# Hybrid decoder step on one core: rate products of layer 0 at earlier steps, two state stores moved behind the last

## The reference, cut to what matters

```python
mod = (silu(c) @ w_ada[0] + b_ada[0])        # shift, scale, gate rates: 6 x 2048 per sequence
sh1, sc1, g1, sh2, sc2, g2 = split_cols(mod, [D_MODEL] * 6)
h = rms_norm(x, norm_mix) * (1 + sc1) + sh1
z = h @ ev_w_in                              # 2048 x 4112
q, k, v, r, a_lr, u = split_cols(z, ...)
o, s_new = gated_linear_recurrence(q, k, v, log_a, s)   # s: one 128 x 256 state per head, 4 heads
p = multiscale_pool(u, ...)                  # windows 2, 4, 8, 16, then a 256 x 256 product per group
x = x + g1 * (concat([rms_norm(o) * silu(r), p]) @ ev_w_out)
```

## Time and profile before

| | |
|---|---|
| median of 3 runs | 2540.3 us (2539.91 to 2542.41) |
| profiled execution, its own time | 2540.4 us |
| its span (first to last instruction) | 2538.6 us |
| PE / PEld busy | 2498.6 us (98%) / 2420.8 us (95%) |
| DVE / ACT / POOL busy | 1509.9 / 985.5 / 157.5 us |
| DMA over the span | 620.50 MB, mean 244 GB/s |
| mean granted TensorE clock | 0.996 |

### The profile page before, as it was taken

The page is one execution under the profiler, slowest core; times in us unless marked ns, Lnnn a source line. Parts: engine busy times, 40 slices in busy tenths (PEclk is TensorE's granted clock), DMA queues, the critical chain, the costliest instruction groups (busy, mean ns, idle before and its releaser), DMA issues.

```text
span 2538.6 us, 59285 instructions
## 1 busy us (share of the span) xinstructions
PE 2498.6 (98%) x24993; PEld 2420.8 (95%) x24993; DVE 1509.9 (59%) x2265; ACT 985.5 (39%) x1144; POOL 157.5 (6%) x211
## 2 busy tenths in 40 slices
PE   7999999999999999999999999999999999999998
PEld 6888799999999999999999999999999999999998
DVE  4575555554454455445548999996755654654654
ACT  3243343332333332333335565656433333333333
POOL 1000331000000000000020020300000000000011
PEclk9999999999999999999999999999999999999999
DMA  9999989899999998998655474745555555555553
GB/s 351 371 353 323 325 303 311 274 311 313 302 311 304 307 309 299 307 307 296 221 182 176 156 245 159 254 153 167 172 178 181 182 179 174 178 181 182 177 175 130
DMA packets 475913, 620.50 MB, mean 244 GB/s; under 512 B 10871, under 2 KB 375829, under 8 KB 471641
## 3 DMA queue, kind: packets, MB, share of 16 engines
q1 hardware_dynamic: 467682, 591.70, 70.2%
q0 software_dynamic: 8096, 26.84, 3.1%
HBM read 606.62 MB, written 13.29 MB: 244 GB/s over the span
## 4 chain that ended last, share of the span: by engine, by line
PE 92%; DMA 3%; DVE 2%; ACT 2%; issue 1%; SPq 0%; ACTq 0%; DVEq 0%
PE ps L1013 26%; PE ps L1014 26%; PE ps L1015 26%; PE pm L1140 5%; PE ps L1057 2%; DMA wide<-in_w_ada 2%; DMA raw<-in_ev_w_in 1%; PE pm L1122 1%; PE ps L1221 1%; PE ps L1222 1%; PE ps L1223 1%; DVE w_lo L2284 1%; PE pm L1160 1%; PE pm L1342 1%; ACT w_hi L1712 1%
## 5 line engine op out<-in xcount | busy, mean ns | idle before, releaser
L2284 DVE TENSOR_TENSOR w_lo<-raw,w_hi 128x1024 fp32r<-128x1024 f32 x700 | 867.4, 1241 | 840.1 <-ACT w_hi L1712 833.6
L1712 ACT ACTIVATE w_hi<-raw 128x1024 fp32r<-128x1024 f32 x688 | 726.8, 1058 | 1208.7 <-PE ps L1015 1179.1
L1013 PE MATMUL ps<-h_hi,w_hi 128*128 128x264 f32 x3552 | 1025.2, 289 | 4.5 <-issue 1.6
L1014 PE MATMUL ps<-h_lo,w_hi 128*128 128x264 f32 x3552 | 1013.0, 285 | 0.0
L1015 PE MATMUL ps<-h_hi,w_lo 128*128 128x264 f32 x3552 | 1011.2, 285 | 0.0
L1013 PEld LDWEIGHTS ps<-h_hi,w_hi 128*128 128x128 f32 x3552 | 671.0, 189 | 18.0 <-issue 13.0
L1014 PEld LDWEIGHTS ps<-h_lo,w_hi 128*128 128x128 f32 x3552 | 669.2, 188 | 1.5 <-issue 0.8
L1015 PEld LDWEIGHTS ps<-h_hi,w_lo 128*128 128x128 f32 x3552 | 669.5, 188 | 0.0
L1013 PE MATMUL ps<-f_hi,w_hi 128*128 128x264 f32 x2048 | 584.2, 285 | 0.0
L1014 PE MATMUL ps<-f_lo,w_hi 128*128 128x264 f32 x2048 | 584.2, 285 | 0.0
L1015 PE MATMUL ps<-f_hi,w_lo 128*128 128x264 f32 x2048 | 583.1, 285 | 0.0
(11 more groups left out here) (423 smaller groups left out, 1669.8 us busy)
## 6 DMA issues: line engine op xcount, KB each, us to landing
raw<-in_mlp_w_up SPq DMA_DIRECT2D x128, 1024.0 KB, 5.9
raw<-in_mlp_w_down SPq DMA_DIRECT2D x128, 1024.0 KB, 5.3
wide<-in_w_ada SPq DMA_DIRECT2D x104, 1024.0 KB, 8.9
wide_late<-in_w_ada SPq DMA_DIRECT2D x56, 1024.0 KB, 9.3
raw<-in_od_w_in SPq DMA_DIRECT2D x48, 1024.0 KB, 5.2
raw<-in_ev_w_in SPq DMA_DIRECT2D x32, 1024.0 KB, 10.0
araw<-in_w_ada SPq DMA_DIRECT2D x24, 1024.0 KB, 8.9
raw<-in_ev_w_out SPq DMA_DIRECT2D x16, 1024.0 KB, 6.0
```

The lines of the kernel that those rows point to most:

```text
L1013: nc.tensor.matmul(acc, w_hi[:, slot, cols], xh[:, k, :], start=(k == UK * ends[0]), stop=False)
L1014: nc.tensor.matmul(acc, w_hi[:, slot, cols], xl[:, k, :], start=False, stop=False)
L1712: nc.scalar.activation(w_hi[:, u, :], raw[:, p, u, :], ACT.Copy).then_inc(hi_ready, 1)
L2284: nc.vector.tensor_tensor(w_lo[:, p, u, :], raw[:, p, u, :], w_hi[:, u, :].bitcast(F32), ALU.subtract).then_inc(lo_ready, 1)
```

## The change

Six of the sixteen rate products are put one or two steps earlier on PE: numbers 8 to 13 run behind t = 15, 18, 22, 25, 29 and 32, before behind 17, 20, 23, 26, 30 and 33 (8 and 9 by two steps, 10 to 13 by one). The stores of samples 3 and 4 are issued behind that of sample 7. POOL waits for the stores of samples 1 and 7 before it loads `pool_w`, and for those of 2 to 6 before its window sums; DVE's wait for all seven stands later, behind its sums over the past and one addition. The program of SP is not in the diff.

```diff
--- before.py
+++ after.py
@@ -91,7 +91,8 @@
     return QUARTERS * (w // 2) + (SH1 if w % 2 else SC1)
 
 
-RATES_AT = dict(zip((0, 1, 2, 4, 6, 8, 10, 12, 17, 20, 23, 26, 30, 33, 36, 39), range(16)))
+RATES_AT = dict(zip((0, 1, 2, 4, 6, 8, 10, 12, 15, 18, 22, 25, 29, 32, 36, 39), range(16)))
+LATE_STORES = (3, 4)
 TURNS_AT = {14: 0, 40: 1}
 DOUBLED = (16, 20, 22, 33, 37, 39)
 PACE = [2 if step in DOUBLED else 1 for step in range(45) if step - 1 not in DOUBLED] + [1, 1, 1]
@@ -891,10 +892,15 @@
                     pool.wait_ge(values_in[0], 16 * (2 * q - 1))
                     spread(2)
                 yield
+
+                def store(b):
+                    pool.dma_start(dst[b, hsl].rearrange("h k v -> k h v"),
+                                   state(q, b).rearrange("p (h v) -> p h v", h=HG)).then_inc(st_out[b % nb], 16)
+
                 for b in range(NS):
                     pool.wait_ge(st_ready, NS * q + b + 1)
-                    pool.dma_start(dst[b, hsl].rearrange("h k v -> k h v"),
-                                   state(q, b).rearrange("p (h v) -> p h v", h=HG)).then_inc(st_out[b % nb], 16)
+                    if q or b not in LATE_STORES:
+                        store(b)
                     if b < nb - at_once:
                         load(at_once + b)
                     if q and b == 1:
@@ -905,6 +911,9 @@
                         pool.wait_ge(st_out[(b - 2) % nb], 16 * transfers(q, b - 2))
                         load(b - 2 + nb)
                     yield
+                if q == 0:
+                    for b in LATE_STORES:
+                        store(b)
 
             def prompt_state(q):
                 h = HEADS[q]
@@ -925,13 +934,14 @@
                 if i == 6:
                     pool.wait_ge(small_out, 16)
                     pool.dma_start(pastu[:, :], io["state_pool"][0].rearrange("b r c -> (b r) c")).then_inc(past_in, 16)
-            for b in range(NS - HEADS[0]["bufs"], NS):
+            for b in (1, NS - 1):
                 pool.wait_ge(st_out[b % HEADS[0]["bufs"]], 16 * transfers(0, b))
             pool.wait_ge(o8_psum, NS)
             pool.dma_start(pool_w[:, :, :, :], io["ev_pool_w"][0].rearrange("g (c p) e -> p g c e", p=P)).then_inc(aw_in, 16)
 
             pool.wait_ge(evacuated, 12)
-            pool.wait_ge(o8_psum, NS)
+            for b in range(2, NS - 1):
+                pool.wait_ge(st_out[b], 16 * transfers(0, b))
             u = z[:, 24:32, 0:TP]
             for g, w in enumerate(WINDOWS):
                 src, width, bufs = u[:, 2 * g:2 * g + 2, :], 1, [pa, pb]
@@ -2793,8 +2803,6 @@
                 yield
                 dve.wait_ge(past_psum, 1)
                 dve.wait_ge(evacuated, 12)
-                for b in range(NS - HEADS[0]["bufs"], NS):
-                    dve.wait_ge(st_out[b % HEADS[0]["bufs"]], 16 * transfers(0, b))
                 for g, w in enumerate(WINDOWS):
                     b = g // 2
                     c0 = (g % 2) * 240
@@ -2804,6 +2812,8 @@
                 yield
                 dve.wait_ge(past_taken, 1)
                 step(nc.vector.tensor_tensor(t8[:, 0:8, :], t8[:, 0:8, :], z[:, 24:32, TP:T], ALU.add))
+                for b in range(NS - HEADS[0]["bufs"], NS):
+                    dve.wait_ge(st_out[b % HEADS[0]["bufs"]], 16 * transfers(0, b))
                 for g, w in enumerate(WINDOWS):
                     last = nc.vector.scalar_tensor_tensor(z[:, 32 + 2 * g:34 + 2 * g, TP:T], t8[:, 2 * g:2 * g + 2, :], 1.0 / w,
                                                           z[:, 24 + 2 * g:26 + 2 * g, TP:T], ALU.mult, ALU.subtract)
```

## The result

The changed kernel takes 2555.09 us (median of 6 runs, 2551.59 to 2557.17) against 2539.75 us before (6 runs): a ratio of 1.0057, 95% interval 1.0044 to 1.007. It is slower, as forecast, by 15.3 us where 9.3 were forecast; the time lies near the upper end of the range, and above the 2545.4 to 2553 us of the forecast proper. The profiled execution took 2555.88 us with a span of 2554.1. From here on the stage between the two `mod_rows` turns of PE (t = 14 and t = 40) is the yardstick. Its length comes from single profiles, but it leaves out what the runs vary by before it.

A forecast was written before the change was run, and what follows sets the result against it. PE was taken to bound the kernel, with a 4.66 us hole behind t = 30. Waits of 6.1 and 5.0, a gain of 4.1, stores 0 and clock 2.3 gave +9.3 us: 2549.7 us, range 2543.5 to 2556.

The forecast's parts named there:

- Products 8 and 10: Rate products moved to behind t = 15 and t = 22 on PE: no wait expected, cost nothing.
- B: PE's wait behind t = 25 for the rows of rate product 11: cost 5.0 us, 2.6 with a quiet landing.
- A: PE's wait behind t = 18 for the rows of rate product 9: cost 6.1 us, bounds 5.0 and 6.6.
- C: Hole behind t = 30: idle 4.66 to 2.1 us and half clock gone, -4.1 us; bounds -2.6 and -6.2.
- Late stores: Two 512 KB stores leaving the late weight half's stretch: alone worth 2.7 us, beside the moved products nothing.
- the hole: PE's idle time of 4.66 us behind t = 30, in front of the turn of the samples' answers.
- D: Late stores meeting later engine work behind t = 30: cost 0, bounds 0 and 2 us; landing by 7 to 9.6 us.
- one of the signs of being wrong: Among the signs: PE waiting for the rows of rate 13 or for POOL's sums.
- The rival "heavier": Late stores also meet rate 13: D = 2, B at 5.5, a third clock drop; 2554 us, chance 0.15.
- The sum: 6.1 + 5.0 - 4.1 + 0 + 2.3 = +9.3 us for the whole change.
- Clock: Half clock on PE around A and B: 1.5 and 0.8 us, together 2.3, bounds 0 and 4.5.

The follow-up runs named there:

- move_8_9: The kernel before with rate products 8 and 9 alone moved (behind t = 15 and 18); 2548.0 us, ratio 1.003 to before.
- reordered: The changed kernel with SP's list of requests put in the order of the new steps; 2536.86 us, ratio 0.999 to before.
- ten_at_23: The changed kernel with rate product 10 put back behind t = 23; 2552.08 us, ratio 1.0049 to before.
- late_1_to_4: The changed kernel with the stores of samples 1 and 2 late as well as 3 and 4; 2557.42 us, one run.
- reordered_cover: The reordered kernel with products 12 and 13 and SP's request of rates 14 placed as before the change; 2536.02 us, ratio 0.9987 to before.
- rates_only: The changed kernel with no late stores, rate products still moved; 2555.77 us, ratio 1.0066 to before.
- late_5_6: The kernel before with the stores of samples 5 and 6 late, POOL's and DVE's waits adapted; 2536.02 us, ratio 0.9984 to before.

## Why the prediction was right, and where its sizes were off

**Products 8 and 10: right.** No wait in front of product 8, of the copies behind t = 17, or of product 10. But product 10 was not free: see B.

**A: right, its sum in part by luck.** Forecast 6.1 us and 1.5 of clock, measured 7.4 in all (in move_8_9 the stage is 7.3 longer). The landings forecast 8.3 and 11.7 us behind the weight half came at 8.1 and 10.5. With these the second half ends only 5.0 us late at full clock (240.04 + 0.93, against 234.09 + 1.85), the lower bound, and the clock cost 2.3 us instead of 1.5: two errors that nearly cancel. SP's place in its list was the cause: the DMA engines had room on both sides of the wait, and reordered removed it.

**B: the mechanism right, the size wrong.** This is the step that failed: "It is the same place with the same loads and stores beside it". Forecast 5.0 us and 0.8 of clock, measured 10.5. With landings of 13.2 and 16.9 us the second half ends 7.9 us late at full clock (286.13 + 0.93, against 277.35 + 1.85); the rest, 2.6 us, is clock, half for 10.2 us in the trace. The landings were later because product 10 was moved, which ten_at_23 shows. The move put POOL's first store and its load of sample 6 ahead of the weight half; that this order delayed the rows fits all the rows read here but isn't shown apart from SP's closer requests. I had moved each rate product's PE time and its rows, but not the transfers of another queue that hang on what stands behind it on PE.

**C: right but for the clock.** The idle was forecast 2.1 and is 2.23, ACT began right behind the unit (312.37) and no longer waited for the DMA. But half clock came back behind 2.23 us of idle (315.10 to 320.00 at 0.65), so C is -2.3 and not -4.1; the bound given, -2.6, was for just this. That it came back is not settled by the 2.23 us: in ten_at_23 and late_1_to_4 it didn't. The reading that product 12 was the cover is confirmed by reordered and reordered_cover.

**Late stores: half right.** Beside the moved products they gain nothing: right (rates_only). Alone they were said to be worth 2.7 us of the hole; they were worth 4.1 and the clock, less 1.5 before the pooling. D was forecast 0 with 2 as its bound, and is 1.2: the two stores, issued at 311.33 and 312.08, took 11.5 us each and landed at 322.8 and 323.6, 10.6 and 11.4 us behind the end of unit t = 30 (312.2), both beyond the 9.6 allowed. POOL's sums began 11.7 us behind that end, not 8.8, and took 32.3 us (323.93 to 356.26) where they took 30.5 before; with either alone they would have been ready when PE came at 355.08. So one of the signs of being wrong that the prediction named, PE waiting for POOL's sums, did show. The rival "heavier" is what happened in kind (D, B longer than forecast and a third drop of clock) and it gave 2554 us, 1 from the measured time; but the rows of rate 13 weren't late.

**The sum.** The parts measured add up to 16.8 us, 7.5 more than the 9.3 forecast: 4.7 of that are B's (10.5 for 5.8), 1.8 C's, 1.2 D's, and A is 0.2 under. That the time still lies inside the range is in part luck. The stage's 16.9 us on the 2540.4 of the prediction would be 2557.3 us, above the range; PE entered the stage 1.5 us sooner in the changed kernel's profile, and that entry lies anywhere from 215.3 to 217.4 in the twelve kernels.

**Clock and queues.** The clock was half for 6.8 us about t = 18 and for 10.2 us about t = 25, and cost 2.3 and 2.6 us, where 1.5 and 0.8 were forecast. The Trainium skill (TensorE: Matmul & The Clock Gate, section HAM oscillation) says that PE falls back to half clock when short bursts of matmuls stand between long waits for DMA. By it both A and B pay in full; the trace agrees.

At t = 25 POOL's queue moved 1 MB more beside the same 3.4 MB of SP's. The Trainium skill (DMA: Bandwidth & Descriptors, section Queues, rings and completion order) says that a DMA engine takes packets in turn from the queues that have work. That fits these figures, though no run here shows the turns themselves; the prediction weighed it only for rate 13, where nothing waited.

## What to carry to other kernels

A consumer that moves earlier has to take its producer's request along: where requests stand in one list in program order, find the line whose wait will hold the request in the new order, and compare the landing with the new time of use. Then look which requests wait for a unit ahead of the moved step and which for one behind it, since transfers of another queue can change places with your own. And what seems mere work next to a hole may be the cover of a second wait behind the first; ask what it hides before it is moved.

## What the runs showed that was not expected

- An idle time of 2.23 us was followed by half clock in three kernels (changed, rates_only, reordered) and not in late_1_to_4 or ten_at_23; one of 2.28 us (late_5_6) was not either. The length of one wait alone doesn't decide it; whoever sizes it has to keep both cases.

```profile
297.10:300.20 3.10, 3.10 (x26) 3.10 (x27) 0.22 (x1) 0.00 (x0) 0.00 (x0) 1.00 1.00 399
...
298.00:302.00 4.00, 4.00 (x21) 4.00 (x22) 0.23 (x1) 0.00 (x0) 0.00 (x0) 0.57 1.00 418
```

The first row is late_5_6 behind its 2.28 us, the second reordered behind its 2.23 us.

- 1 MB of stores issued ahead of a weight half, in full engines, cost that half 5.6 us of landing, twice its bytes over the bandwidth; 1 MB issued behind it cost 2.4 us (16.6 and 14.2). Why the first is twice stays open.
